# Latent attention's entry on one core: two column pieces, late normalisation, rotations and a residual's scale moved between engines

## The reference

```
cq, ckv, kr = split(h @ w_down, [256, 512])          # 1024 -> 256 + 256 + 32
q  = (rms_norm(cq,  q_norm)  @ w_uq ).reshape(16 heads, 64 + 32);  q_rope = rope(q[..., 64:])
kv = (rms_norm(ckv, kv_norm) @ w_ukv).reshape(16 heads, 64 + 64);  k_rope = rope(kr)  # one for all heads
s  = (q_nope . k_nope + q_rope . k_rope) * 96 ** -0.5;  o = softmax(s) @ v;  out = o @ w_out
rms_norm(x, w) = x * rsqrt(mean(x * x) + 1e-6) * w
```

## Time and profile before

| | us |
|---|---|
| median of 3 timed runs | 1075.19 (1074.13 to 1075.66) |
| span of the profiled execution | 1072.5 |
| TensorE busy | 1028.6 |
| VectorE busy | 797.6 |
| ScalarE busy | 495.1 |
| GpSimd busy | 73.0 |

### The profile page before, as it was taken

One profiled execution on the slowest core, in us unless ns is written; L12 is line 12 of the kernel. 1 busy time (PEld: TensorE's weight loads), 2 busy tenths in 40 slices (PEclk: granted clock), 3 DMA queues, 4 the chain that ended last, 5 costly groups with the idle time before them and its releaser, 6 DMA issues.

```text
span 1072.5 us, 13324 instructions
## 1 busy us (share of the span) xinstructions
PE 1028.6 (96%) x5104; PEld 857.2 (80%) x5104; DVE 797.6 (74%) x1147; ACT 495.1 (46%) x721; POOL 73.0 (7%) x161
## 2 busy tenths in 40 slices
PE   8899999999998999999999999999988899999996
PEld 7788888789976778888887888888878777888885
DVE  5678889777797687888778778877756677666455
ACT  2443434446767453434435344443456554434340
POOL 1000000001311000000000000000441000000000
PEclk9799999999999999999999999999899999999999
DMA  9899999736332489979848988972223338666531
GB/s 370 338 338 357 365 379 385 254 120 210 111 119 89 157 327 350 325 271 344 292 152 339 322 306 279 382 267 82 85 79 118 119 136 305 230 229 219 196 118 39
DMA packets 72321, 254.80 MB, mean 238 GB/s; under 512 B 8769, under 2 KB 10049, under 8 KB 72258
## 3 DMA queue, kind: packets, MB, share of 16 engines
q1 hardware_dynamic: 68946, 242.91, 62.8%
q0 software_dynamic: 3168, 10.52, 3.1%
q10 hardware_dynamic: 144, 0.52, 0.2%
HBM read 252.85 MB, written 1.07 MB: 237 GB/s over the span
## 4 chain that ended last, share of the span: by engine, by line
PE 79%; DVE 9%; issue 3%; ACT 3%; DMA 3%; POOL 1%; SPq 0%; DVEq 0%; ACTq 0%; POOLq 0%
PE bank L1600 24%; PE bank L1604 24%; PE bank L1603 24%; DVE w_lo L1039 3%; DMA w_raw<-in_w_dram 2%; PE bank L1966 2%; ACT w_hi L768 1%; PE bank L1914 1%; PE bank L1703 1%; PE bank L1726 1%; DMA w_raw<-in_ada_w_dram 1%; POOL arena L722 1%; PE bank L1693 1%; ACT arena L783 1%; PE bank L1595 1%
## 5 line engine op out<-in xcount | busy, mean ns | idle before, releaser
L1039 DVE TENSOR_TENSOR w_lo<-w_raw,w_hi 128x2048 fp32r<-128x2048 f32 (+2 forms) x162 | 355.5, 2216 | 28.3 <-ACT w_hi L768 28.3
L1600 PE MATMUL bank<-w_hi,hT_hi 128*128 128x512 f32 (+3 forms) x880 | 353.1, 401 | 4.3 <-DVE hT_lo L1078 4.3
L1604 PE MATMUL bank<-w_lo,hT_hi 128*128 128x512 f32 (+3 forms) x880 | 343.5, 390 | 0.0
L1603 PE MATMUL bank<-w_hi,hT_lo 128*128 128x512 f32 (+3 forms) x880 | 342.8, 390 | 0.0
L768 ACT ACTIVATE w_hi<-w_raw 128x2048 fp32r<-128x2048 f32 (+2 forms) x162 | 300.2, 1856 | 37.0 <-DMA w_raw<-in_w_dram 29.7
L1600 PEld LDWEIGHTS bank<-w_hi,hT_hi 128*128 128x128 f32 x880 | 168.7, 192 | 35.1 <-DVE hT_lo L1078 3.6
L1604 PEld LDWEIGHTS bank<-w_lo,hT_hi 128*128 128x128 f32 x880 | 168.2, 191 | 34.4
L1603 PEld LDWEIGHTS bank<-w_hi,hT_lo 128*128 128x128 f32 x880 | 168.8, 192 | 30.4
L838 ACT ACTIVATE arena<-bank 128x256 f32<-128x256 f32 x88 | 33.7, 383 | 313.2 <-PE bank L1604 313.2
L1050 DVE SCALAR_TENSOR_TENSOR arena<-arena,c_row 128x1024 f32<-128x1024 f32 x136 | 161.9, 1220 | 9.0 <-DMA cols<-in_cols_dram 8.1
L1600 PE MATMUL bank<-w_hi,fT_hi 128*128 128x512 f32 x352 | 138.3, 393 | 3.6 <-DVE fT_lo L1533 3.6
(11 more groups left out here) (231 smaller groups left out, 876.1 us busy)
## 6 DMA issues: line engine op xcount, KB each, us to landing
w_raw<-in_w_dram SPq DMA_DIRECT2D x310, 512.0 KB, 5.3
arena<-in_ada_w_dram SPq DMA_DIRECT2D x140, 512.0 KB, 7.1
gate_row<-gate_scratch POOLq DMA_DIRECT2D x6, 512.0 KB, 4.8
arena<-in_ln_g_dram POOLq DMA_DIRECT2D x6, 512.0 KB, 5.0
arena<-in_ln_b_dram POOLq DMA_DIRECT2D x6, 512.0 KB, 7.6
w_raw<-in_w_dram SPq DMA_DIRECT2D x8, 256.0 KB, 2.9
w_raw<-in_w_dram SPq DMA_DIRECT2D x8, 192.0 KB, 2.8
gate_row<-in_ada_w_dram SPq DMA_DIRECT2D x2, 512.0 KB, 12.9
```

What stands on the lines that cost most here:

```text
L1039: nc.vector.tensor_tensor(w_lo[:, j0 % RING, 0:n], w_raw[:, j0 % RAW, 0:n], w_hi[:, j0 % RING, 0:n].bitcast(F32), ALU.subtract)\
L1600: mm = nc.tensor.matmul(dst, a_hi, b_hi, start=start, stop=False)
L1603: nc.tensor.matmul(dst, a_lo, b_hi, start=False, stop=False)
L1604: return nc.tensor.matmul(dst, a_hi, b_lo, start=False, stop=stop)
```

## The change

The down projection is done in two pieces that each hold whole tokens' columns: `kv`, the 256 columns of the latent keys and values, and `cq`, the 256 of the queries together with the 32 of the rotated key (288 columns). The weights are laid out to match, in three slots of 2048, 2016 and 288 columns; the earlier ones had 2048, 2048 and 256. ScalarE copies each piece out of PSUM unscaled and squares it with an accumulator. The transposes are taken of the unscaled copies. The rms factor, a number per token, multiplies at the evictions of `uq` and `ukv`; the attention scale moves from there to the copy of the transposed queries. Rotations are done on VectorE with three or four small operations and a sum. `scale` moves to GpSimd. The key's copy now comes ahead of the query's and `M_KEYS` counts more finely. The plan is reordered.

```diff
-            yield from (("c", (0, 0)), ("lo", 2), ("cq", 0), ("enter", 1), ("cn", 0), ("kr", (0, 0)), ("c", (0, 1)),
-                        ("scale", 0), ("split", 3), ("rot", 0), ("hi", 4), ("cq", 1), ("cn", 1), ("cT", 0), ("kr", (0, 1)),
-                        ("lo", 4), ("hi", 5), ("cT", 1), ("uq", (0, 0)), ("ukv", (0, 0)), ("lo", 5), ("scale", 1),
-                        ("uq", (0, 1)), ("qkT", (0, 0)), ("ukv", (0, 1)), ("hi", 6), ("uq", (1, 0)),
-                        ("qkT", (0, 1)), ("lo", 6))
+            yield from (("kv", (0, 0)), ("kv_out", 0), ("rot", 0), ("lo", 2), ("cq", (0, 0)), ("enter", 1), ("cq_out", 0),
+                        ("split", 3), ("kr", 0), ("rms", 0), ("kv", (0, 1)), ("cT", 0), ("cn", (0, 0)), ("cn", (0, 1)),
+                        ("scale", 0), ("split", 4), ("cq", (0, 1)), ("kv_out", 1), ("scale", 1), ("cq_out", 1), ("uq", (0, 0)),
+                        ("kr", 1), ("cT", 1), ("rms", 1), ("ukv", (0, 0)), ("cn", (1, 0)), ("hi", 5), ("uq", (0, 1)), ("cn", (1, 1)),
+                        ("lo", 5), ("qkT", (0, 0)), ("ukv", (0, 1)), ("hi", 6), ("uq", (1, 0)), ("qkT", (0, 1)), ("lo", 6))
...
-        M_KEYS = {0: 4, 4: 8, 8: 12, 10: 16}
+        M_KEYS = {0: 3, 2: 4, 4: 7, 6: 8, 8: 11, 10: 15, 14: 16}
...
 # GpSimd
+                        elif stage == "scale":
+                            t = m
+                            pool.wait_ge(ln_rows_in, 32 * s)
+                            pool.wait_ge(n_tr, 2 * (2 * s + t) + 2)
+                            step(nc.gpsimd.tensor_tensor(x[:, t, :], x[:, t, :], ln_rows[:, 0, :], ALU.mult))
+                            step.wait()
+                            nc.gpsimd.tensor_tensor(x[:, t, :], x[:, t, :], ln_rows[:, 1, :], ALU.add).then_inc(x_ready, 1)
...
 # ScalarE
+                        elif stage in ("kv_out", "cq_out"):
+                            t, v = m, int(stage == "kv_out")
...
+                            nc.scalar.activation(c_nat[:, t, M_FIRST[v]:M_FIRST[v] + width], bank[:, 0:width], ACT.Copy)                                .then_inc(c_out, 1)
+                            nc.scalar.activation(bank[:, 256:512] if v else cq_square[t], bank[:, 0:256], ACT.Square,
+                                                 accum_out=ssq[:, 2 * t + v:2 * t + v + 1]).then_inc(proj_read, 1)
+                        elif stage == "cn":
+                            t, v = m
+                            act.wait_ge(c_tr, 2 * t + v + 1)
...
+                            for n in range(2):
+                                k = 2 * v + n
+                                op = nc.scalar.activation(hT_hi[:, k, t * P:(t + 1) * P], c_bank(t, v)[:, n * P:(n + 1) * P],
                                                           ACT.Copy, scale=norm_col[:, k:k + 1])
+                            op.then_inc(c_hi, 1)
                         elif stage == "uq":
...
+                                act.wait_ge(rms_ready, R0 + t + 1)
                             nc.scalar.activation(q_nat[:, t, :, :], mla_bank(stage, m)[:, 0:384].rearrange("p (h n) -> p h n", h=4),
-                                                 ACT.Copy, scale=MLA_SCALE).then_inc(proj_read, 1)
+                                                 ACT.Copy, scale=rms[:, 2 * t:2 * t + 1]).then_inc(proj_read, 1)
...
 # VectorE
-                    elif stage == "scale":
-                        scale_shift(s, m)
...
+                        for n in range(2):
+                            k, tok = 2 * v + n, slice(t * P, (t + 1) * P)
+                            op = nc.vector.scalar_tensor_tensor(out=hT_lo[:, k, tok], in0=c_bank(t, v)[:, n * P:(n + 1) * P],
+                                                                scalar=norm_col[:, k:k + 1], in1=hT_hi[:, k, tok].bitcast(F32),
+                                                                op0=ALU.mult, op1=ALU.subtract)
+                        op.then_inc(cT_ready, 1)
...
+                    elif stage == "uq":
+                        g, t = m
+                        dve.wait_ge(proj_read, P0 + mla_piece(stage, m) + 1)
...
+                        step(nc.vector.tensor_tensor(rp[:, 0, :, :], part, rot[:, 0, t:t + 1, :].broadcast_to([P, 4, 32]), ALU.mult))
+                        for c, src in ((slice(0, 16), slice(16, 32)), (slice(16, 32), slice(0, 16))):
+                            step(nc.vector.tensor_tensor(rp[:, 1, :, c], part[:, :, src],
+                                                         rot[:, 1, t:t + 1, c].broadcast_to([P, 4, 16]), ALU.mult))
+                        step.wait()
+                        nc.vector.tensor_tensor(q_nat[:, t, :, 64:96], rp[:, 0, :, :], rp[:, 1, :, :], ALU.add)\
+                            .then_inc(q_rot, 1)
...
 # TensorE
+                    elif stage in ("kv", "cq"):
+                        t = m[1]
+                        width = 256 if stage == "kv" else M_CQ
...
+                        if g == 0:
+                            pe.wait_ge(cT_ready, 2 * t + v + 1)
...
+                        else:
+                            pe.wait_ge(cT_ready, 4)
+                        for bank, src in ((banks[7], k_nat), (banks[6], q_nat)):
```

More of the change, by code:

```diff
@@ L714, in _ @@
                 if kind == "mla":
[L716 to L727, removed]
                     for stage, m in mla_plan():
-                        if stage == "cq":
+                        if stage == "rms":
                             t = m
@@ L1651, in mla @@
                         enter(s + 1, 0)
+                    elif stage in ("kv", "cq"):
+                        t = m[1]
+                        width = 256 if stage == "kv" else M_CQ
+                        bank = mla_bank(stage, m)
+                        for k in range(KD):
+                            if stage == "kv":
+                                j0, at = base[s], k
+                                if k % 2 == 0:
+                                    pe.wait_ge(h_ready, 4 * (2 * s + t) + k // 2 + 1)
+                            else:
+                                j0, at = base[s] + 1 + k // 7, k % 7
+                            if t == 0 and at == 0:
+                                slot_wait(j0)
+                            w, tok = slice(at * width, (at + 1) * width), slice(t * P, (t + 1) * P)
+                            mm = product(bank[:, 0:width], hT_hi[:, k, tok], hT_lo[:, k, tok],
+                                         w_hi[:, j0 % RING, w], w_lo[:, j0 % RING, w], k == 0, k == KD - 1,
+                                         owed(s) if (stage, t, k) == ("kv", 0, 0) else None)
+                        mm.then_inc(proj_done, 1)
                     elif stage in M_SLOT:
@@ new lines, in mla @@
+                        j0 = base[s] + M_SLOT[stage] + 2 * g
+                        if t == 0:
+                            slot_wait(j0)
+                        for k in range(2):
+                            w, tok = slice(k * width, (k + 1) * width), slice(t * P, (t + 1) * P)
+                            mm = product(bank[:, 0:width], hT_hi[:, 2 * v + k, tok], hT_lo[:, 2 * v + k, tok],
+                                         w_hi[:, j0 % RING, w], w_lo[:, j0 % RING, w], k == 0, k == 1)
@@ L1684, in mla @@
+                        pe.wait_ge(proj_read, P0 + 2)
+                        for v in range(2):
+                            for n in range(2):
+                                c = M_FIRST[v] + n * P
+                                mm = nc.tensor.transpose(c_bank(m, v)[:, n * P:(n + 1) * P], c_nat[:, m, c:c + P], ident[:, :])
+                            mm.then_inc(c_tr, 1)
                     elif stage == "qkT":
@@ L1690, in mla @@
                             pe.wait_ge(qk4_ready, 2 * (2 * g + t))
-                        for bank, src in ((banks[6], q_nat), (banks[7], k_nat)):
+                        else:
+                            pe.wait_ge(cT_ready, 4)
+                        for bank, src in ((banks[7], k_nat), (banks[6], q_nat)):
                             for h in range(4):
@@ L2055, in latent @@
         down, uq, ukv = (np.asarray(inputs[f"mla_w_{k}"])[0] for k in ("down", "uq", "ukv"))
-        yield from columns(down, 0, 512)
-        yield tiles(down[:, 512:544])
+        yield tiles(down[:, 256:512])
+        queries = tiles(np.concatenate([down[:, 0:256], down[:, 512:544]], axis=1))
+        yield queries[:, 0:7 * 288]
+        yield queries[:, 7 * 288:]
         for g in range(4):
```

166 lines of the change are left out of this document (67 added, 99 removed).

## The result

The changed kernel takes 1080.22 us (median of 5, 1078.49 to 1081.86), the kernel before beside it 1075.19 (5 runs). The ratio is 1.0059, 95% interval 1.0042 to 1.0076. That is slower, by 5.0 us between the two medians and by 6.3 us by the ratio (4.5 to 8.2), where 1.1 us faster was forecast. The profiled execution took 1079.58 us.

What follows compares the result with a forecast made beforehand. TensorE, 96% busy, was taken to bound the kernel. Scale and lead 1.8, rotations -1.3 and -0.3, finer key waits 0.9 sum to 1.1 us faster than 1075.19: 1074.1 us, range 1070 to 1078.8.

Steps and rivals of the forecast that it cites:

- What bounds it: Whole kernel: TensorE, 96% busy, sets the pace; time is won only where it waits or does needless work.
- narrow pieces: Latent down projection: 256- and 288-column matmuls save 4.0 us of TensorE's time, a lead of 4.4 us after the first ukv.
- The residual's scale: Latent entry: four operations on GpSimd, 2.0 us each, delay the second factor to 775.5, leaving 1.8 us won of 4.4.
- the term of 2.6 us: Latent entry: the part of the 4.4 us lead that moving the scale to GpSimd would cost.
- my bound from above: Shared port in the entry: VectorE's small operations wait up to 4 x 2.0 us less gaps, some 6 us.
- Rival (b): Latent entry: each GpSimd scale operation holds VectorE, TensorE stands and restarts at half clock; 2.4 us slower, 1077.6; chance 0.24.
- its threshold of 2.2 us: Scale on GpSimd: the length per operation from which, with two intrusions, the slower rival decides.
- The sentence that nothing else stood in the way: Factor at eviction: its VectorE and ScalarE changes stood outside the gap; balance zero, from 1 us won to 0.5 lost.
- rival (a): Latent entry: the port hardly matters, second factor at 773.0, clock stays up; 3.7 us faster, 1071.5; chance 0.27.
- Rotations, -1.3 and -0.3: VectorE's in-order queue: group 1's rotations delay the second transposes' copies by 1.3 us and the second scores' maximum by 0.3.
- Keys first, 0.9: Attention scores: waiting for the key copy alone wins 0.9 us, bounds 0 and 1.9.

Runs made afterwards that it cites:

- e1: Changed kernel with the residual's gain and bias left out altogether, GpSimd only signalling: ratio 1.0006 to the kernel before.
- e5: e4 with c's second half, its mean square and ukv(0,1) earlier in the plan, and the scale's second half moved: ratio 0.9989 to the kernel before.
- e6: e4 with the rotations of groups 1 to 3 moved later in VectorE's queue alone: ratio 1.0003 to the kernel before.
- e4: Changed kernel with the residual's scale back on VectorE at the same two places of the plan: ratio 1.0024 to the kernel before.
- e11: Kernel before with only the rotations of queries and keys moved from GpSimd to VectorE: ratio 0.9992.
- e12: e4 with the rotations on GpSimd instead of VectorE: ratio 0.9981 to the kernel before.
- e10: Kernel before with only the key bank transposed and copied first and scores waiting for the key copies alone: ratio 0.9987.
- e13: e9 with the four pieces of the scale on GpSimd at the same places of the plan: ratio 0.9976 to the kernel before.
- e2: Changed kernel with each of GpSimd's four scale operations cut into four of 256 columns, same place in its queue: ratio 1.0046 to the kernel before.
- e7: Kernel before with only the residual's scale moved from VectorE to GpSimd at the same two places: ratio 1.0055.
- e15: Changed kernel with the rotations back on GpSimd, beside the residual's scale: ratio 1.0024 to the kernel before.
- e3: Changed kernel with all four scale operations moved behind the second half's factor in GpSimd's queue: ratio 1.0083 to the kernel before.
- e14: e13 with each of the four scale pieces cut into four operations of 256 columns: ratio 0.9987 to the kernel before.
- e9: Changed kernel with scale on VectorE in four pieces, c's second half earlier, late rotations, first scores' maximum first: ratio 0.9916 to the kernel before.

## Why the prediction was wrong

**What bounds it, narrow pieces: right.** 256 columns start 0.12 apart, 288 0.133, both as worked out. The first ukv ends 19.0 us after the entry's start, against 24.2 before by the prediction's count (775.2 - 750.96): 5.2 us of lead where 4.4 were forecast, and up to 1.4 more if the clock stayed up, as it did (1.00).

**The residual's scale: the step that failed.** Forecast was that "VectorE's split of slot 4 waits behind it", and that the other three operations pass "with gaps and the small rotations between", 2.0 us each, so that the late factor on GpSimd would be last, at 775.5. The split did wait (2.80 us instead of 1.21). But the three small rotation instructions were held for 2.25, 2.50 and 2.31 us, one behind each other, and the term of 2.6 us (4.4 of lead down to 1.8) measured 5.7 (changed against e1). Three things were off. The operation takes 2.34 to 2.40: the 64-column row of the same kind gives 2.3, and I took 2.0. VectorE's instruction waited for what was left of GpSimd's, and each row of the rotation met another one: I counted that for the split and not for the rotation, though my bound from above, "some 6 us", had it. (What lets GpSimd's next operation in isn't shown: the rotation's products don't wait for each other, only its sum waits for them.) And the forecast's timeline has full-clock lengths behind a wait of TensorE of some 5 us: transposes 0.85 and ukv 1.4, measured 1.57 and 2.70 from start to start.

The Trainium skill, SBUF — State Buffer, "Who interferes with whom", says of VectorE's two-port modes that whoever issues first keeps the shared pair for the whole instruction and the other is fully blocked; of a tensor_tensor with both inputs in SBUF it says that it contends with GpSimd's reads. The trace shows the same full blocking for those, at 2.25 to 2.50 us a row.

**Rival (b) was the mechanism.** "TensorE has stood since 770.8 and restarts at half clock": it stood from 769.5 to 776.3, for VectorE's c, and restarted at 0.50. (b) gave 1077.6, by 2.4 us of loss; the loss was 5.0. It had the second transposes end at 785.1; they end at 787.4, with an entry that starts 0.56 us sooner. Between lie a wait of 2.21 us ahead of the first transposes and a clock that I let rise too soon (means 0.65, 0.50 and 0.64 from 769.4 to 786.2); no run separates the two. I gave (b) 0.24, because I put the operation under its threshold of 2.2 us; the 2.3 from the earlier trace rows stands over it already.

**The sentence that nothing else stood in the way: wrong.** e1 has no scale and wins nothing (1.0006), where rival (a) would have had 3.7 us. The lead went into two gaps of 2.09 and 2.21 us, because ScalarE makes c's second half only after it has evicted ukv, and VectorE only after the rotation. I had costed the factor at eviction at zero. e5 changes the order of the plan alone and wins 3.8 us.

**Rotations, -1.3 and -0.3: right in place, not in size.** VectorE waits 3.56 us for the eviction behind the split of slot 6 and copies the keys only at 788.40; TensorE waits 1.69. Moving them late wins 2.2 us (e6); taking them off VectorE wins 4.6 in e4's plan, nothing in that of before (e11, e12). The maximum of the second scores, costed at 0.3, stands behind a rotation that waits for ScalarE: in e1 it starts at 788.12, 37.3 us after the entry's start, before at 787.82 or 36.9. The lead of 1.1 us that e1 has at the first scores is gone there.

**Keys first, 0.9:** 1.4 measured alone (e10), with an interval from -0.1 to 2.8 us. Not told apart from what was forecast.

**Range:** 1070 to 1078.8 missed by 1.4 us, as it allowed "half a microsecond to one" for the clock beyond (b), whose loss was 2.6 us larger.

What stays open: why the rotations on VectorE cost 4.6 us in e4, when the traces show 2.4 at the first scores and the later steps take the other 2.2; no run separates the clock from the queue there. And how e13's 6.4 us divide between the held instructions and the clock. And whether the narrow pieces win anything on the kernel before by themselves: no run has them alone.

## What to carry to other kernels

Work moved off a busy engine is only free if the engine that takes it shares nothing with the first: here 5 us of VectorE work cost 3.8 us more on GpSimd than where it was. Look for two prices. One is the new engine's queue: whatever small thing on the path stands behind the work there comes late (e2, e7, e15). The other is what the two engines share: each small VectorE instruction beside it can lose up to the length of one GpSimd operation (the changed kernel, e3, e13), and cutting the operation up won nothing clear of the noise (e2, e14). And when a part of the path gets shorter, look at once at what the order behind it assumed: with scale and rotations on VectorE the change's own plan gave nothing (e4), and 9.0 us under the kernel before with its queues re-sorted (e9).

## What the runs showed of the hardware

- Not only two-operand instructions are held. A tensor_scalar on two columns of SBUF took 1.91 us (e7), 2.35 (e15) and 0.68 (e2) instead of 0.16 beside GpSimd's operations, about their length. The Trainium skill, SBUF — State Buffer, "Who interferes with whom", counts tensor_scalar among the operations that can take the shared pair; the trace agrees, down to two columns. Instructions with an operand in PSUM were not, where the traces have them: c's subtraction takes 0.60 to 0.61 a pair with GpSimd at work (e2, 772.24) and without, and the copies of the transposes 1.28 with it (e7, 778.74) and 1.29 without (e7, 786.00).
- It holds both ways. GpSimd's add of 1024 columns took 3.26 us instead of 2.34 where VectorE's split came first (766.73), and two products of 64 columns 2.56 instead of 0.60 (e12).
- TensorE's clock: after 6.8 us of idle time it was at 0.50 through 6.1 us (776.3 to 782.4) although TensorE worked 3.9 of them. After 1.37 us (ahead of 759.17, in the same trace) it stayed at 1.00. In e1 two gaps of 2.1 and 2.2 us come with 0.66; in e5 one gap of 2.06 with 1.00. A gap's price is then more than its length in some places and not in others, by what stands around it. Nor is idle time needed: before, the clock was 0.50 with TensorE busy all of 3 us, just behind the 32-column matmuls; in the changed kernel, where 256 and 288 columns stand there, it is 1.00 to 769.4.
- Lengths by row: GpSimd 128x1024 in float32, two operands, 2.34 to 2.40 us, and about 0.7 a piece of 256; VectorE's version 1.22.
